# Moving the sample tile's retention behind the first gather, strips to ScalarE and a one-hot product to GpSimd

## The chip, the cores and the metric

The kernel runs on one core of one Trainium2 chip. The metric is the device time of one execution in microseconds (us), taken as the median of three runs.

## The reference

One layer of a streaming encoder is computed for two request groups that share the weights: a prompt of 1024 tokens and 8 running streams with 16 new tokens each (the "sample" group, 128 tokens), with 1024 features.

```python
h = rms_norm(x, norm1_g)
rq, rk, rv, rg, fq, fk, fv, logf = project(h, w_in, ...)   # 7 x 512 columns, and 8
ro, s_new = retention(rq, rk, rv, s0)                      # 8 heads of 64, recurrent state
fo = fox_block(...)                                        # softmax attention, 8 heads of 64
x = x + combine(ro, rg, fo, ret_out_g, fox_out_g, w_out)   # norms, swish gate on ro, w_out
x = x + peer(rms_norm(x, norm2_g), peer_wq, peer_keys, peer_u, peer_v)
...
def peer_tokens(x, wq, keys, u, v):      # per token and head: 16 experts out of 16384
    ... v1, i1 = lax.top_k(s1, 16); v2, i2 = lax.top_k(s2, 16)
    cv, ci = lax.top_k(v1 + v2 (all pairs), 16)
    e = i1[ci // 16] * 128 + i2[ci % 16]; g = softmax(cv)
    act = gelu(x . u[e]);  return sum over heads and experts of g * act * v[e]
```

For the prompt the retention state starts at zero and runs through all tokens; for the sample group each of the 8 streams starts from its own state (`state_ret`, 8 x 8 heads x 64 x 64) and returns a new one. The expert lookup needs 8 x 16 rows of `peer_u` and of `peer_v` for each of 1152 tokens: 8 KB for each expert and token, 1208 MB in all.

## The kernel before, in words

The 1152 tokens are nine tiles of 128: tiles 0 to 7 are the prompt, tile 8 (`ST`) is the sample group. The program has five parts, one after the other.

1. `phase_norm`: x is normalized and transposed to `hT` for all nine tiles, and the retention queries RQ are projected for the tiles in `EARLY`.
2. `projection([RK, RV], ...)`: retention keys and values of the tiles in `EARLY`. A projection of one tile to 512 columns is 16 matmul records on TensorE (PE).
3. `phase_retention`: scores, causal mask, outputs, state and swish gate of the tiles in `EARLY`, and the forget logits of all tiles.
4. `projection([FQ, FK, FV], ...)`: the softmax attention's q, k, v for tiles 0 to 2.
5. `phase_tail`: the rest, in two layers that run beside each other. The **stream** works token by token through all 1152 tokens. GpSimd (POOL) issues one indirect DMA per token (L1914, 1 MB each) into a ring of nine slots. VectorE (DVE) takes the dot products with u (L2842). After each four tokens ScalarE (ACT) computes a tanh (L2130) for the gelu, DVE forms the 128 x 32 x 4 block of weights called strips in two instructions (`exg` L2859, `strips` L2864), and PE multiplies it with v (L2468), which frees four ring slots (`uv_free`). The **fronts** are everything else for three groups of tiles, 0 to 2, 3 to 5, 6 to 8: projections, retention of the tiles not in `EARLY`, attention, output projection, query and key scores (rq, rscore), top-16 searches (rtop) and the choice of the experts (rcand, 27 steps per tile, rexp, rmove). Front 0 lies before the first gather; front 1 must have chosen tile 3's experts before gather 384 and front 2 tile 6's before gather 768.

Each engine's queue is in order. `front_steps()` writes the front steps down as two threads (`rest`, `choice`), each step with a cost per engine and the steps it needs. `deal()` plays the steps against a model of the stream once, when the program is built, and so fixes between which gathers, dots, tanhs and multiplications each step is put (`due`). A front step on an engine is a companion of the stream.

In the kernel before, `RETAINED = {1: [3, 4, 5], 2: [6, 7]}`: tiles 3 to 5 get their retention in front 1, tiles 6 and 7 in front 2, and `EARLY` is tiles 0, 1, 2 and 8. Tile 8 has a step of its own in `phase_retention` (`outputs_sample`, then `turn_sample`), and its new states are made in four pieces in the steps of tiles 1 and 2 (`state_sample`, `add_state`); its 128 x 512 retention output goes to HBM (`rets`) and is read back by `sload` in front 2, beside the things that the sample attention needs. The gate weights of that phase are loaded in its beginning, and tile 0's outputs come before its gate matmuls there. In the choice, for each of tiles 1 to 8 DVE four times compares the candidates with an iota to a one-hot block of 128 x 1024 (L2604), multiplies it with the positions (L2608) and sums it (L2611).

## Time and profile before

| | |
|---|---|
| median of 3 runs | 3679.78 us (3669.91 to 3693.92) |
| profiled execution, own time | 3684.22 us |
| its span, first to last instruction | 3682.4 us |
| PE / DVE / ACT / POOL busy | 64% / 66% / 13% / 38% |
| DMA moved | 1363.76 MB, 370 GB/s over the span |
| first gather issued, last gather issued | 443.8 us, 3663.2 us |

Times in the rows below are us from the start of the span unless marked ns. The profile is one execution; its own time, 1.8 us above its span, is 4.4 us above the median of the runs.

### The profile page before, as it was taken

To read this page: it belongs to the slowest core of one execution; us is meant where nothing else is said; L and a number is where in the kernel's file an instruction comes from. 1 tells how busy PE (TensorE), PEld (TensorE's weight loads), DVE (VectorE), ACT (ScalarE), POOL (GpSimd) and SP (SyncE) were. 2 spreads that over 40 slices of the span, in tenths; PEclk is the share of its full clock that TensorE was granted. 3 is DMA by queue.
4 is the path that set the end of the run, shared out by engine and by line. 5 is a ranking of instruction groups with operands and counts; after the bars stand their busy time and mean duration, and the time that the engine had idled before them with its cause. 6 is when DMAs were issued, how large, how long until landed. Compare 5 with 4: busy or idle time off the path is not lost.

```text
span 3682.4 us, 32200 instructions
## 1 busy us (share of the span) xinstructions
PE 2344.0 (64%) x10543; PEld 926.8 (25%) x10543; DVE 2422.2 (66%) x6345; ACT 494.6 (13%) x1368; POOL 1403.2 (38%) x1276
## 2 busy tenths in 40 slices
PE   7997885758677678667747877788443343334333
PEld 3544431313333233122213444233100000000000
DVE  3232479886666559888765566578988765565555
ACT  1113211011022111011101122111101100000000
POOL 0010033533444434444343344434544444444443
PEclk9998997879778789778857678799665665656555
DMA  3145289999999999999999999999999999999998
GB/s 145 41 143 199 93 346 406 413 390 401 418 407 401 409 400 415 397 408 423 401 400 404 383 384 404 417 401 414 411 403 418 419 417 418 417 420 420 417 420 370
DMA packets 227782, 1363.76 MB, mean 370 GB/s; under 512 B 34384, under 2 KB 53720, under 8 KB 76064
## 3 DMA queue, kind: packets, MB, share of 16 engines
q0 software_dynamic: 165888, 1208.03, 79.9%
q1 hardware_dynamic: 61440, 153.08, 11.0%
q8 instruction: 84, 1.38, 0.1%
q10 hardware_dynamic: 288, 0.59, 0.0%
q14 instruction: 82, 0.67, 0.0%
HBM read 1336.77 MB, written 24.85 MB: 370 GB/s over the span
## 4 chain that ended last, share of the span: by engine, by line
DMA 39%; PE 24%; DVE 13%; POOL 9%; issue 6%; ACT 1%; POOLq 0%; DVEq 0%; ACTq 0%
DMA M<-in_peer_uv,M 39%; PE yp L2468 12%; POOL M L1914 8%; DVE M L2842 6%; PE ab L2416 2%; PE ab L2233 1%; PE ab L2178 1%; PE d L2213 1%; DVE exg L2859 1%; DVE strips L2864 1%; PE ef L2450 1%; PE d L2395 1%; PE c L2201 1%; DVE gel L2851 1%; PE c L2395 1%
## 5 line engine op out<-in xcount | busy, mean ns | idle before, releaser
L1914 POOL DMA_INDIRECT M<-in_peer_uv,M x1152 | 1302.9, 1131 | 1819.6 <-PE yp L2468 1477.9
L2842 DVE SCALAR_TENSOR_TENSOR M<-M 128x1024 f32<-128x1024 f32 x1152 | 1407.7, 1225 | 780.8 <-DMA M<-in_peer_uv,M 752.7
L2468 PE MATMUL yp<-M,strips 128*32 128x512 f32 x4608 | 861.5, 886 | 1092.5 <-DVE strips L2864 1065.9
L2468 PEld LDWEIGHTS yp<-M,strips 128*32 128x32 f32 x4608 | 154.7, 141 | 1680.2 <-DVE strips L2864 1310.0
L2130 ACT ACTIVATE gel<-gel 128x4 f32<-128x4 f32 x288 | 59.2, 206 | 1997.9 <-DVE gel L2853 1979.5
L2416 PE MATMUL ab<-M 128*128 128x512 f32 x576 | 264.6, 608 | 4.1 <-ACT M L2084 4.1
L2233 PE MATMUL ab<-M 128*128 128x512 f32 x320 | 148.4, 614 | 0.0
L2416 PEld LDWEIGHTS ab<-M 128*128 128x128 f32 x576 | 107.9, 195 | 147.2 <-issue 142.7
L2291 PE MATMUL ab<-M 128*128 128x512 f32 x288 | 133.2, 614 | 5.7 <-DVEq L2635 5.6
L434 PE MATMUL z<-M 128*128 128x512 f32 x272 | 120.6, 600 | 0.9 <-PEq L105 0.9
L2656 DVE CUSTOM_DVE_ANT_0 M<-ab,M 128x896 f32<-128x896 f32 (+6 forms) x64 | 48.4, 756 | 91.4 <-PE ab L2179 70.6
L2864 DVE SCALAR_TENSOR_TENSOR strips<-gel,exg 128x128 f32<-128x128 f32 x288 | 84.1, 292 | 33.4 <-ACT gel L2130 23.2
L2201 PE MATMUL c<-ident,M 128*128 128x128 f32 x288 | 56.7, 313 | 65.4 <-ACT M L1952 41.7
L2842 DVE DVE_READ_ACCUMULATOR M<-M 128x1 f32 x1152 | 95.0, 82 | 0.0
L2859 DVE TENSOR_TENSOR exg<-e,gel 128x128 f32<-128x128 f32 x288 | 84.1, 292 | 10.0
L2213 PE MATMUL d<-M 128*64 128x128 f32 x576 | 88.7, 307 | 0.9 <-ACT M L1960 0.9
L2178 PE MATMUL ab<-M 64*128 64x512 f32 (+3 forms) x192 | 86.3, 560 | 3.8 <-DVE mins L2656 3.8
L2233 PEld LDWEIGHTS ab<-M 128*128 128x128 f32 x320 | 60.6, 197 | 87.6 <-issue 84.9
L2450 PE MATMUL ef<-M,ident 128*32 128x512 f32 x576 | 76.1, 664 | 5.7 <-ACT M L2126 3.5
L2213 PEld LDWEIGHTS d<-M 128*64 128x64 f32 x576 | 72.3, 155 | 17.3 <-issue 15.0
L2291 PEld LDWEIGHTS ab<-M 128*128 128x128 f32 x288 | 54.5, 196 | 81.5 <-issue 81.5
L1939 ACT ACTIVATE M<-M,mins 128x896 f32<-128x896 f32 (+6 forms) x64 | 49.6, 775 | 150.6 <-DVE mins L2656 146.4
(305 smaller groups left out, 2511.7 us busy)
## 6 DMA issues: line engine op xcount, KB each, us to landing
M<-in_c_win SPq DMA_DIRECT2D x20, 2048.0 KB, 11.4
M<-in_c_wq SPq DMA_DIRECT2D x12, 2048.0 KB, 12.2
M<-in_peer_uv,M POOLq DMA_INDIRECT x1152
M<-in_w_out SPq DMA_DIRECT2D x24, 512.0 KB, 8.6
M<-in_x_prompt SPq DMA_DIRECT2D x16, 512.0 KB, 11.2
x_scratch<-M SPq DMA_DIRECT2D x9, 512.0 KB
M<-x_scratch SPq DMA_DIRECT2D x9, 512.0 KB
out_y_prompt<-M SPq DMA_DIRECT2D x8, 512.0 KB
```

Source lines behind the costliest of these rows:

```text
L434: last = nc.tensor.matmul(z[n % 3][:, :], hT[:, k, t * P:(t + 1) * P], wbuf[:, slot(gi), k, :], start=(k == 0), stop=(k == KC - 1))
L1914: nc.gpsimd.indirect_dma_start(ring[n % NR], None, a["peer_uv"], bass.IndirectOffsetOnAxis(ap=idxH[:, t % 6, s // 4, s % 4:s % 4 + 1], axis=0)
L2178: nc.tensor.matmul(s[:, c:c + w], rows_q[b0:b0 + 64, r], rows_k[b0:b0 + 64, r, c:c + w], start=True, stop=c + w < width)
L2213: last = nc.tensor.matmul(Dk[b0:b0 + 64, 0:P], (vg if g else vn)[:, j, h * HD:(h + 1) * HD], pT[:, n % 2, j, :], start=(j == 0), stop=(j = ...
L2233: last = nc.tensor.matmul(half_ab[j % 2], l_h[i][:, k, :], pw[q % 2][:, k, :], start=(k == 0), stop=(k == KC - 1))
L2291: last = nc.tensor.matmul(half_ab[j % 2], l_h[i][:, k, :], f_pw(q)[:, k, :], start=(k == 0), stop=(k == KC - 1))
L2416: last = nc.tensor.matmul(half_ab[i % 2], xT[:, tt, k, :], wq(g, b)[:, k, :], start=(k == 0), stop=(k == KC - 1))
L2450: last = nc.tensor.matmul(EF[32 * b:32 * b + 32, half, :], ident[:, 32 * j:32 * j + 32], xb[:, 512 * half:512 * half + 512], start=True, s ...
L2468: last = nc.tensor.matmul(yp[32 * j:32 * j + 32, 512 * c:512 * c + 512], strips[:, n % 2, j, :], ring[(4 * n + j) % NR][:, D + 512 * c:D + ...
L2842: nc.vector.scalar_tensor_tensor(out=row, in0=row, scalar=1.0, in1=xrep[:, s % 4, :], op0=ALU.mult, op1=ALU.mult, accum_out=dots[:, t % 2, ...
L2859: link(nc.vector.tensor_tensor(exg[:, :, :], bc(e32[:, :].unsqueeze(1), [P, 4, 32]), bc(g[:, 3, :].unsqueeze(2), [P, 4, 32]), ALU.mult))
L2864: nc.vector.scalar_tensor_tensor(out=strips[:, n % 2], in0=bc(g[:, 2, :].unsqueeze(2), [P, 4, 32]), scalar=1.0, in1=exg[:, :, :], op0=ALU. ...
```

## The change

Tile 8's retention leaves the phases ahead of the tail and becomes part of front 2: `RETAINED[2]` is 6, 7, 8 and `EARLY` is 0, 1, 2. Its projections are four more `lmm` steps, its scores an `lsc`; its outputs come in two halves from an initial state loaded from HBM in another layout (`lxo`), are turned back (`lback`), and its new states are made in four pieces (`lvbd`, `lnew`) and written to HBM by ACT's queue. The sample attention's small loads move into the second `sload`, behind the last state piece, while the first two pieces of its key and value caches keep their place ahead of the outputs. `rets` goes. In `phase_retention` tile 0's gate matmuls come before its outputs, and the weights FQ are loaded in its beginning. In the stream the strips are made by ACT, in four activations of 128 x 32 with a scale from memory, after one 128 x 4 instruction of DVE. In the choice of tiles 1 to 8 the product L2608 goes to POOL; DVE waits for it (`picked`) before the sum. Some semaphores are merged, and the planner's costs are adapted. The diff, cut to its core:

```diff
-        RETAINED = {1: [3, 4, 5], 2: [6, 7]}
+        RETAINED = {1: [3, 4, 5], 2: [6, 7, 8]}
...
                 for s, t in enumerate(ORDER):
-                    whole = s == 0 or t == ST
...
-                    if t == ST:
-                        outputs_sample()
...
+                def across(half):
+                    add(rest, ("lxo", g, half), pe=(6.1, ("sp", ("sload", g, 0)), ("dve", ("lsc", g, NL - 1)), ("act", ("lval", g, 3 * NL - 1)),
+                                                    *(bank("A", "act", ("lxo", g, 1)) if half == 0 else [])),
+                        **({"act": (0.7, ("pe", ("lxo", g, 1)))} if half else {}))
+                def renew(r):
+                    add(rest, ("lnew", g, r), pe=(1.3, ("dve", ("lvbd", g, r)), *bank("DB"[r % 2], "dve", ("lnew", g, r))),
+                        dve=(1.2, ("pe", ("lnew", g, r)), ("pe", ("lxo", g, 1))), act=(0.3, ("dve", ("lnew", g, r))))
...
+                if len(prompt) < NL:
+                    across(0)
+                    gated(0, "lout")
+                    across(1)
+                    renew(0)
+                    gated(1, "lout")
+                    add(rest, ("lback", g), pe=(0.75, ("act", ("lxo", g, 1)), *bank("C", "act", ("lback", g))), act=(1.5, ("pe", ("lback", g))))
+                    renew(1)
+                    spread(2)
+                    gated(2, "lback")
+                    renew(2)
+                    spread(3)
+                    renew(3)
...
+                    if g == SG:
+                        routed += [("dve", ("lnew", g, PAIRS - 1))]
...
-                        add(rest, ("sprep", g, p), dve=(1.3, ("sp", ("sload", g, 0))))
+                        add(rest, ("sprep", g, p), dve=(1.3, ("sp", ("sload", g, 1))))
...
+                        if p in PICKED:
+                            add(choice, ("rcand", g, i, p), pool=(2.2, ("dve", ("rcand", g, i, p - 1))))
...
+                    elif kind == "lxo":
+                        half, n = arg[0], NKEPT[g] + len(RETAINED[g])
...
+                        for h in range(4 * half, 4 * half + 4):
+                            b0, r = 64 * (h % 2), h // 2
+                            o = four(half_ab[0])[b0:b0 + 64, r, :]
+                            nc.tensor.matmul(o, l_v[-1][:, h * HD:(h + 1) * HD], l_sT[-1][:, h % 2, r, :], start=True, stop=False)
+                            for b in range(NB):
+                                c = slice(b * NS, (b + 1) * NS)
+                                last = nc.tensor.matmul(o[:, c], l_s0[r][b0:b0 + 64, b, :], l_qT[-1][b0:b0 + 64, r, c],
+                                                        start=False, stop=(b == NB - 1))
...
                 def gelu_tanh(n):
                     act.wait_ge(gel1, n + 1)
                     nc.scalar.activation(gel[:, n % 2, 2, :], gel[:, n % 2, 1, :], ACT.Tanh).then_inc(gel2, 1)
...
+                    if n >= 2:
+                        act.wait_ge(uv_free, n - 1)
+                    act.wait_ge(gel3, n + 1)
+                    for j in range(4):
+                        last = nc.scalar.activation(strips[:, n % 2, j, :], e32[:, :], ACT.Copy, scale=gel[:, n % 2, 3, j:j + 1])
+                    last.then_inc(strip_done, 1)
...
-                    link(nc.vector.tensor_tensor(exg[:, :, :], bc(e32[:, :].unsqueeze(1), [P, 4, 32]),
-                                                 bc(g[:, 3, :].unsqueeze(2), [P, 4, 32]), ALU.mult))
                     dve.wait_ge(gel2, n + 1)
-                    if n >= 2:
-                        dve.wait_ge(uv_free, n - 1)
-                    nc.vector.scalar_tensor_tensor(out=strips[:, n % 2], in0=bc(g[:, 2, :].unsqueeze(2), [P, 4, 32]),
-                                                   scalar=1.0, in1=exg[:, :, :], op0=ALU.add, op1=ALU.mult
-                                                   ).then_inc(strip_done, 1)
+                    nc.vector.scalar_tensor_tensor(out=g[:, 3, :], in0=g[:, 2, :], scalar=1.0, in1=g[:, 3, :],
+                                                   op0=ALU.add, op1=ALU.mult).then_inc(gel3, 1)
```

## Rows read from the trace of the kernel before

**Rows 1.** Busy times by stage: three stretches of five parts, us.

```profile
69.20:129.20 60.00, 58.81 (x144) 26.31 (x144) 10.95 (x20) 4.69 (x8) 0.00 (x0) 0.97 0.09 35
...
129.20:216.50 87.30, 82.13 (x470) 42.04 (x470) 32.66 (x55) 9.13 (x16) 7.87 (x9) 0.98 0.31 88
...
644.00:3682.40 3038.40, 1818.80 (x8496) 681.57 (x8496) 2119.17 (x5425) 367.73 (x1046) 1292.73 (x1149) 0.73 0.99 407
```

**Rows 2.** DMA queues from the first gather to the end: packets, MB, share.

```profile
q0 software_dynamic: 165888, 1208.03, 90.8%
q1 hardware_dynamic: 30480, 102.69, 8.0%
```

**Rows 3.** The chain of waits late in the stream: start, us, what.

```profile
3220.14 10.05 DMA M<-in_peer_uv,M
...
3232.61 3.68 PE yp L2468 x16
```

**Rows 4.** PE's timeline where the first part ends and the second begins.

```profile
55.87 8.80 PE L298 MATMUL z<-M 128*128 128x512 f32 x16 [0.83 <-ACT M L194]
...
69.26 1.40 PE L434 MATMUL z<-M 128*128 128x512 f32 x2 [0.93 <-PEq L105]
```

**Rows 5.** PE's timeline in the retention phase.

```profile
135.14 1.89 PE L686 MATMUL op<-M 128*128 128x64 f32 x16
...
139.62 7.13 PE L759 MATMUL z<-M 128*128 128x512 f32 x16 [1.98 <-DMA M<-in_c_win]
146.69 1.16 PE L673 MATMUL sc<-M 64*128 64x128 f32 x16
...
169.61 1.16 PE L673 MATMUL sc<-M 64*128 64x128 f32 x16
...
180.73 1.08 PE L741 MATMUL opT<-M 128*64 128x512 f32 x4
...
183.92 1.58 PE L741 MATMUL opT<-M 128*64 128x512 f32 x4 [1.05 <-DVE M L841]
```

**Rows 6.** DMA queue q1 from 188 to 207 us (new states written).

```profile
q1 hardware_dynamic: 4435, 1.56, 33.0%
```

**Rows 7.** Groups of instructions in the stream by line and shape.

```profile
L2864 DVE SCALAR_TENSOR_TENSOR strips<-gel,exg 128x128 f32<-128x128 f32 x288 | 84.1, 292 | 33.4 <-ACT gel L2130 23.2 <-DVE exg L2859 0.9
L2859 DVE TENSOR_TENSOR exg<-e,gel 128x128 f32<-128x128 f32 x288 | 84.1, 292 | 10.0
...
L2130 ACT ACTIVATE gel<-gel 128x4 f32<-128x4 f32 x288 | 59.2, 206 | 1997.9 <-DVE gel L2853 1979.5 <-issue 17.9
...
L2857 DVE SCALAR_TENSOR_TENSOR gel<-dots,M 128x4 f32<-128x4 f32 x288 | 44.8, 156 | 0.0
...
L2608 DVE TENSOR_TENSOR M<-M 128x1024 f32<-128x1024 f32 x34 | 41.5, 1221 | 0.2
```

**Rows 8.** Groups of POOL over the whole span.

```profile
L1882 POOL TENSOR_TENSOR psm<-psm,nhalf 128x8 f32<-128x8 f32 x12 | 23.9, 1992 | 1.0
...
L888 POOL MEMSET M<- 128x512 f32 x1 | 0.5, 524 | 77.3 <-POOLq L105 77.3
```

**Rows 9.** Busy times in two stretches where the experts are routed.

```profile
1343.00:1743.00 400.00, 275.15 (x1132) 103.10 (x1132) 339.58 (x1108) 56.47 (x160) 171.31 (x151) 0.83 1.00 412
...
2412.00:2641.00 229.00, 158.00 (x654) 61.66 (x652) 191.66 (x628) 27.33 (x72) 96.91 (x86) 0.85 1.01 413
```

**Rows 10.** POOL's timeline, gather 384.

```profile
1564.06 1.01 POOL L1914 DMA_INDIRECT M<-in_peer_uv,M  x1 [2.82 <-ACT M L1966]
```

**Rows 11.** ACT's timeline, tile 6's experts moved.

```profile
2636.74 4.27 ACT L1966 CAST M<-M 32x32 int32<-32x32 f32 x16
```

**Rows 12.** POOL's timeline, gather 765 (gather 768 is the third after it).

```profile
2686.95 0.95 POOL L1914 DMA_INDIRECT M<-in_peer_uv,M  x1 [4.31 <-PE yp L2468]
```

**Rows 13.** Retention projections of front 2: count, first and last start.

```profile
L2233 PE MATMUL ab<-M x128: 592/592/1223, 1737.9 to 1841.0; 128*128 128x512 f32 x128
```

**Rows 14.** PE's timeline, third piece of the sample's keys.

```profile
1936.22 1.97 PE L2330 MATMUL ab<-ident,M 128*128 128x128 f32 x8 [7.48 <-DMA M<-in_c_ck]
```

More of the change, by code:

```diff
@@ L678, in outputs @@
                 def outputs(t):
-                    s = AT[t]
                     o = op[t % 2]
@@ L2617, in choose @@
                                             ).then_inc(csub, 1)
-                chosen = {}
+                chosen, taken = {}, [0]
                 def front(step):
```

512 lines of the change are left out of this document (251 added, 261 removed).

## The prediction

> **What bounds the kernel now.** I read the busy times by stage first. The span falls in two. Ahead of the first gather, to 443.8 us, PE is the full engine: it is busy 58.8 of 60.0 us in the key and value projections and 82.1 of 87.3 us in the retention phase, with the DMA engines at 0.09 and 0.31 [rows 1]. From 644 us on the DMA share is 0.99 at 407 GB/s, while PE is busy 60% and DVE 70% [rows 1]. Next the DMA queues over the stream's 3238.6 us: the gathers alone hold the 16 engines 90.8% of it, 2941 us, and everything else 8.0%, 259 us [rows 2]. That leaves about 39 us, or 1.2%, for idling and small descriptors. So the stream lasts as long as its bytes do, whatever DVE and PE have spare. The chain of waits says it in its way: late in the stream the last gather of four takes 10.05 us from issue to landing, and PE begins 2.4 us after that [rows 3]; four gathers take 2941/288 = 10.2 us of engine time, so these 10 us are queueing behind other gathers, not distance. Work that is taken from DVE in the stream buys no time by itself. Work that is taken from before the first gather buys all of it, as long as it fits beside the stream.
>
> **The part ahead of the gathers.** First part: tile 8's queries, from 55.87 to 69.26 us [rows 4]. Without them the second part can start once the last transposes are copied (at 55.9) and after the 0.9 us that the border costs: 56.8. This saves 12.4 us. Second part: 8 projections take 60.0 us, 7.5 each with the border [rows 1]; 2 go, and the matmuls themselves take 7.13 + 0.2 at most in the third part [rows 5], so I take 14.6 us. Third part: tile 8's step goes, from 146.69 to 169.61, 22.9 us. Four state pieces go, in two pairs: 1.08 + 1.05 (wait) + 1.58 us, twice, 7.4 us in all [rows 5]. Against that, tile 0's outputs, from 135.14 until PE sat idle at 139.62 - 1.98 = 137.64, 2.5 us, lay in the shade of the load of the gate weights [rows 5]. Now the gate matmuls come first and still wait for that load, and the outputs come after: 2.5 us are given back. Net 27.8 us. The 1 MB of old states and 1 MB of new ones also leave this phase; nothing waited for them, so this is worth nothing here. DVE is busy 33 of 87 us there and can't be next [rows 1]; the weights FQ now come earlier and were not waited for. Sum: 12.4 + 14.6 + 27.8 = **54.8 us**, by which the first gather should come earlier, at about 389 us. Front 0 itself is unchanged.
>
> **What the stream gets: bytes.** New in it: 1.05 MB of old states, 0.52 MB of tile 8's hT, 0.07 MB of constants, less 0.26 MB of `rets`, some 1.4 MB. The other transfers of the stream cost 259 us for 102.7 MB, 2.5 us a MB [rows 2]: 3.5 us. The new states are written in 256-byte pieces: when they were written before, with two `rets`, 4435 packets held the engines 33.0% of 19 us, 6.3 us [rows 6]; 4096 of them are the states, so 5.8 us. The ends are 3.5 us (by bytes alone) and 6.3. Together **+9.3 us** (7 to 10), and these are not hidden, because the engines are full.
>
> **Strips on ACT.** DVE loses two instructions of 0.292 us and gains one like L2857, 0.156 [rows 7]: 0.43 us per group of four tokens, 123 us over 288 groups. ACT gains four activations. The nearest rows are 0.206 us (128x4) and 4.27 us for 16 of 32x32, 0.267 each [rows 7, 11], so 0.8 to 1.1 us a group, some 270 us in all, on an engine that is busy 12% of the stream. On the path from the last dot to PE it adds 0.6 us (0.16 + 0.85 in place of strips' 0.29, less overlap; 0.3 to 1.2). The cover is the queueing of rows 3: when a batch of four is issued, a gather or two is still being moved. I cost it at 0 in the steady state. ACT's queue now holds its next front step behind the wait for DVE's small instruction (`gel3`) and for `uv_free`; both are due within a microsecond of the tanh, which it waited for already. Without the cover it would be 0.6 x 288 = 173 us, which is why the fullness of the DMA matters so much.
>
> **The product on POOL.** It takes 32 x 1.22 = 39 us from DVE [rows 7]. On POOL no row shows a multiplication of 1024. L888 writes 512 numbers in 0.52 us, 1.02 ns each [rows 8]; one pass gives 1.05 us, two reads and a write 3.1 us, and I take 2.2, as one read port's two passes are nearer than either end. L1882 takes 1.99 us for 8 numbers [rows 8], but that is a power. POOL's pause ahead of a batch is 4.31 us in the row of gather 765 [rows 12], so the product fits. Behind it on POOL are gathers, behind the wait for it on DVE are dots. Each engine is in order, so a late batch makes DVE wait for POOL, which waits for PE, up to some microseconds, of which the ring takes the most: 0 to 1 us each, **+3 us** in all (0 to 30). The Trainium skill (GPSIMD Engine Reference, Performance versus the Vector engine) has a two-input tensor_tensor of 2048 fp32 at 4497 ns on GpSimd against 2293 on VectorE. By that it would be an estimated 2.25 us here, and the sum stays as it is; DVE's row, 1.22 us, agrees with its half of the pair.
>
> **Does the last front still come in time?** This decides the rest. Before, the experts of tile 6 are in place at 2636.74 + 4.27 = 2641.0 us, and gather 768, the first to need them, is issued three gathers of 0.95 + 0.3 us after 2686.95, at 2690.7 [rows 11, 12]: 50 us of slack. Tile 3's come with none, gather 384 waits 2.8 us for them [rows 10]. Added to front 2: four `lmm`; the eight of before took 103.7 us, 13.0 each, and no more than one goes into a group of 10.2 us [rows 13]: 41 to 52 us. Two halves of outputs: tile 8's step of 22.9 us holds them beside gate matmuls of 7.1 and scores of 1.2 [rows 5], so they are 14 us at most, and one half fits between two multiplications of the stream: two groups, 20 to 25 us. Four state pieces, each a ping-pong of DVE, PE, DVE, partly side by side: three to six groups, 30 to 60 us. The small loads now start behind them; but the sample attention's third key piece came only at 1936.22, 7.5 us late [rows 14], and that one is queued behind the same values as before, so 0 to 25 us. Together 90 to 160 us, and I take 95, near the lower end, because a state piece is short on PE (1.08 us when its operands are there, [rows 5]) and several fit into one group. Against that: the 9.3 us of bytes delay gather 768 as well; and DVE, busy 85% from 1343 to 1743 and 84% from 2412 to 2641 [rows 9], is what rtop and the choice wait for there, and in the stream's beginning too. Its relief is 0.43 us a group over the 62 groups of these stretches and some 30 of the beginning, 39 us, and 1.22 x 4 for each tile chosen on the way, some 10 us more if POOL keeps up. So front 2 would be later by 95 - 49 = 46 us against the stream, and slack and bytes make 60. It just fits: no stall in the likeliest case, but with a margin of 14 us under an uncertainty of 40.
>
> **The sum.** 3684.2 - 54.8 + 9.3 + 3 = 3641.7 us for the profiled execution; less the 4.4 us by which that stood above the median, 3637. With a few us for idling that a fuller ACT lets through I say **3639 us**.
>
> **Rivals.**
> *The last front is late* (tile 6's experts come after the ring asks for them). For it: the additions above to 160 us and a relief that may be less than 49 if PE, busy 69% in both stretches, sets the pace instead of DVE. Against: 50 us of slack. Point from which it costs: front 2 later by over 60 us. Late by 90, it costs 30 us: 3669. Slower than before begins at about 100 us; at 160 less 20 of relief, 140, the gathers stand still for 80 us, all engines with them: 3719 (+1.1%). That is the case of the other side.
> *POOL and DVE wait for one another.* Here the products are paid with DMA idling. For it: 32 new hand-overs, where L1882's twelve are of the same kind [rows 8]. At 1 us each instead of 0.1: 3639 + 29 = 3668. The Trainium skill (GPSIMD Engine Reference, Specifications) names VectorE instructions with two SBUF inputs as contending with GpSimd, and each dot is one; by that rule the product would stretch by what is left of a dot, 1.2 us, here.
> *The front doesn't shrink as said*, because a load or a barrier holds a part: against it, the DMA share there is 0.09 and 0.31 [rows 1]. Half of the 54.8 us: 3666.
> *Better than forecast*: front 1 no longer late, less idling of the 39 us left over: -10 us, 3627.
>
> **Chances.** Forecast, with up to 5 us either side, 0.42; better 0.10; late front 0.23 with stalls to 45 us and 0.08 beyond; POOL 0.12; front 0.05. A measurement of this kernel can tell about 1%, 37 us: faster by more than that is below 3643. The forecast is mostly there (0.38 of its 0.42), with the better case 0.48, and 0.02 of the others: 0.50. Slower by over 1%, above 3717: half of the last 0.08 and a little, 0.06. Within: 0.44. The range leaves out the long tail of the late front and half of the better case: 3624 to 3692.
>
> **What would show it.** The first gather at 389 us (385 to 394) shows the first sum. 288 groups of four ACT records at 0.2 to 0.25 us, and DVE's L2864 gone, show the strips; the distance from the last dot's landing to PE, 2.4 us, should be 3.0, with gathers still 10 us from issue to landing late in the stream. POOL's product between 1.1 and 3.1 us, and DVE's idle time before its sum under 1 us in the mean, show the third part. Gather 768 should come after POOL's usual wait for PE, not for ACT's moves; if it waits for ACT, the late front is true, and DMA's share falls for that long. The prediction is wrong above all if front 2's relief isn't there, or if the span from first gather to end, 3238.6 us before, grows by more than 20 us.

## The result, and the profile after

The changed kernel takes **3723.35 us** in the median of its four runs, 41 us more than the kernel before beside it (3682.01 us). One run of the four took 8446 us; it is in that median (without it, 3718.52 us) but not in the ratio, which is 1.0108, 95% interval 1.0082 to 1.0133, or some 40 us. Forecast were 3639 us, with a range of 3624 to 3692. The profiled execution took 3714.63 us, its span is 3712.6 us.

The front phases did what was forecast, and a little more. PE's stages for the two remaining projections and for the retention phase, then everything from 585 us on, as rows 1 show it for before (us from start to end and length; PE, PEld, DVE, ACT, POOL busy; clock, DMA share, GB/s):

```profile
56.40:100.50 44.10, 42.93 (x109) 19.23 (x110) 8.20 (x15) 3.51 (x6) 0.06 (x1) 1.00 0.13 48
100.50:159.30 58.80, 54.23 (x268) 27.05 (x268) 18.75 (x32) 6.73 (x12) 5.98 (x7) 0.97 0.21 77
585.00:3712.60 3127.60, 1887.81 (x8746) 722.02 (x8744) 2041.12 (x5145) 626.37 (x2145) 1331.99 (x1181) 0.75 0.98 396
```

The second part takes 44.1 us instead of 60.0, the retention phase 58.8 instead of 87.3 [rows 1]. But the last line is the trouble: 396 GB/s where the kernel before had 407, so the DMA engines, which set the length of the stream, are less full. The queues from the first gather to the end say the same (compare [rows 2]):

```profile
q0 software_dynamic: 165888, 1208.03, 89.0%
q1 hardware_dynamic: 31056, 103.59, 7.8%
q10 hardware_dynamic: 4224, 1.05, 0.1%
```

The same 1208.03 MB of gathered rows hold the engines 89.0% of the stream instead of 90.8%. The stream, from the first gather to the end, is 3327.6 us long instead of 3238.6. Of these 89 us some 61 are idle time of the engines, 8 are the other queues' packets, and 20 are gathered packets that take longer (89.0% of 3327.6 is 2961 us, against 2941 before for the same bytes). In the run with only the retention moved they take 2940 us; why they take longer here is not shown. Where does it fall behind? One row of the gathers' line for each stretch gives the number of gathers in it and the start of its last: 257 gathers, 449, 769 and 865 (counted from 0, the last ones are gathers 256, 448, 768 and 864). First the changed kernel, then the kernel before:

```profile
L1858 POOL DMA_INDIRECT M<-in_peer_uv,M x257: 932/938/2106, 385.0 to 1147.9; - x129
...
L1858 POOL DMA_INDIRECT M<-in_peer_uv,M x449: 932/945/2106, 385.0 to 1753.7; - x150
...
L1858 POOL DMA_INDIRECT M<-in_peer_uv,M x769: 932/944/2106, 385.0 to 2708.0; - x193
...
L1858 POOL DMA_INDIRECT M<-in_peer_uv,M x865: 932/944/2106, 385.0 to 2964.5; - x173
```

```profile
L1914 POOL DMA_INDIRECT M<-in_peer_uv,M x257: 932/938/1974, 443.8 to 1181.5; - x129
...
L1914 POOL DMA_INDIRECT M<-in_peer_uv,M x449: 932/940/2018, 443.8 to 1751.5; - x150
...
L1914 POOL DMA_INDIRECT M<-in_peer_uv,M x769: 932/940/2021, 443.8 to 2691.6; - x193
...
L1914 POOL DMA_INDIRECT M<-in_peer_uv,M x865: 932/946/2021, 443.8 to 2937.9; - x173
```

The first gather is issued 58.8 us earlier. Gather 256 is only 33.6 us ahead, gather 448 is 2.2 us behind, gather 864 is 26.6 us behind. I call what is lost since the first gather the lag: 25 us at gather 256, 61 at 448, 75 at 768, 85 at 864, and 88 at the last (1151). After gather 864 next to nothing is added; there no front is dealt into the stream any more. So the loss is no price per group of four tokens, and not one stall: it gathers in the stretches where VectorE has front work.

The new parts, by line (busy, mean ns of one; then idle time before them and who ended it):

```profile
L2098 ACT ACTIVATE strips<-e,gel 128x32 f32<-128x32 f32 x1152 | 276.1, 310 | 105.1 <-DVE gel L2884 102.6 <-issue 2.4
...
L1839 POOL TENSOR_TENSOR M<-M 128x1024 f32<-128x1024 f32 x32 | 77.9, 2435 | 47.0 <-DVEq L2608 46.7
...
L2884 DVE SCALAR_TENSOR_TENSOR gel<-gel 128x4 f32<-128x4 f32 x288 | 46.8, 163 | 101.4 <-ACT gel L2091 97.7 <-DVE gel L2881 2.0 <-issue 1.7
```

The sizes were forecast well: 276 us for the strips, 2.4 us for a product. The idle columns were not. POOL stands 46.7 us in front of the products, and gathers stand behind it. VectorE waits 97.7 us for the tanh, where `exg` used to cover that time; in the run with only the retention moved, which keeps the old strips, its wait there is 22.7 us. So 75 of the 123 us that the strips took off VectorE came back as waiting.

How long a group holds its slots is seen in the chain of waits late in the stream (start us, us, what):

```profile
3298.86 10.07 DMA M<-in_peer_uv,M
3308.96 1.24 DVE M L2864 x2
3310.22 0.17 DVE gel L2873
3310.42 0.17 DVE gel L2875
3310.61 0.21 ACT gel L2091
3310.92 0.17 DVE gel L2884
3311.18 0.97 ACT strips L2098 x4
3312.19 3.69 PE yp L2470 x16
3315.87 0.26 issue
3316.13 0.94 POOL M L1858
```

The transfer is 10.07 us from issue to landing here too, as in [rows 3]. PE begins at 3312.19, 3.3 us after the landing, against 2.4. From the end of a group's fourth dot to PE's first matmul the median of the 288 groups is 2.01 us, against 1.18 in the kernel before. From the end of the same dot to the end of the group's last matmul, when the slots come free, the mean is 5.85 us, against 4.73.

### The profile page after: what moved, and what is told of

The parts are those of the page before. It is cut to its first block, busy times and chain, and to the rows that moved or that the text cites. A ratio compares the mean times of both kernels' runs of the same rounds, so it can differ in the third digit from the quotient of the medians.

```text
span 3712.6 us, 33319 instructions
## 1 busy us (share of the span) xinstructions
PE 2360.2 (64%) x10537; PEld 943.5 (25%) x10537; DVE 2321.3 (63%) x6025; ACT 762.8 (21%) x2520; POOL 1441.2 (39%) x1308
## 3 DMA queue, kind: packets, MB, share of 16 engines
q0 software_dynamic: 165888, 1208.03, 79.8%
## 4 chain that ended last, share of the span: by engine, by line
DMA 35%; PE 23%; DVE 15%; POOL 8%; issue 6%; ACT 5%; SPq 0%; DVEq 0%; ACTq 0%; another core or an unknown queue 0%; POOLq 0%
DMA M<-in_peer_uv,M 34%; PE yp L2470 11%; POOL M L1858 7%; DVE M L2864 7%; ACT strips L2098 3%; PE ab L2418 2%; PE ab L2201 1%; PE ab L2146 1%; DVE gel L2875 1%; PE d L2181 1%; DVE M L2618 1%; DVE gel L2873 1%; DVE M L2605 1%; PE c L2397 1%; DMA M<-out_new_fox_v_s 1%
## 5 line engine op out<-in xcount | busy, mean ns | idle before, releaser
L1858 POOL DMA_INDIRECT M<-in_peer_uv,M x1152 | 1263.2, 1097 | 1786.6 <-PE yp L2470 1457.5
L2864 DVE SCALAR_TENSOR_TENSOR M<-M 128x1024 f32<-128x1024 f32 x1152 | 1439.3, 1253 | 827.3 <-DMA M<-in_peer_uv,M 807.4
L2098 ACT ACTIVATE strips<-e,gel 128x32 f32<-128x32 f32 x1152 | 276.1, 310 | 105.1 <-DVE gel L2884 102.6
L2418 PE MATMUL ab<-M 128*128 128x512 f32 x576 | 263.5, 605 | 4.1 <-ACT M L2045 4.1
L2201 PE MATMUL ab<-M 128*128 128x512 f32 x384 | 176.8, 613 | 0.0
L2418 PEld LDWEIGHTS ab<-M 128*128 128x128 f32 x576 | 107.3, 194 | 148.3 <-issue 143.8
L2293 PE MATMUL ab<-M 128*128 128x512 f32 x288 | 135.9, 623 | 4.1 <-DVEq L2642 4.1
L2884 DVE SCALAR_TENSOR_TENSOR gel<-gel 128x4 f32<-128x4 f32 x288 | 46.8, 163 | 101.4 <-ACT gel L2091 97.7
L433 PE MATMUL z<-M 128*128 128x512 f32 x240 | 105.0, 593 | 1.4 <-PEq L105 1.4
L2201 PEld LDWEIGHTS ab<-M 128*128 128x128 f32 x384 | 73.0, 196 | 108.0 <-issue 107.6
L1839 POOL TENSOR_TENSOR M<-M 128x1024 f32<-128x1024 f32 x32 | 77.9, 2435 | 47.0 <-DVEq L2608 46.7
```

Source lines behind the costliest of these rows:

```text
L433: last = nc.tensor.matmul(z[n % 3][:, :], hT[:, k, t * P:(t + 1) * P], wbuf[:, slot(gi), k, :], start=(k == 0), stop=(k == KC - 1))
L1839: nc.gpsimd.tensor_tensor(o4, o4, bc(f4[:, q // 16:q // 16 + 4, half, :].unsqueeze(2), [P, 4, TOPK, TOPK]), ALU.mult).then_inc(picked, 1)
L1858: nc.gpsimd.indirect_dma_start(ring[n % NR], None, a["peer_uv"], bass.IndirectOffsetOnAxis(ap=idxH[:, t % 6, s // 4, s % 4:s % 4 + 1], axis=0)
L2098: last = nc.scalar.activation(strips[:, n % 2, j, :], e32[:, :], ACT.Copy, scale=gel[:, n % 2, 3, j:j + 1])
L2201: last = nc.tensor.matmul(half_ab[j % 2], l_h[i][:, k, :], pw[q % 2][:, k, :], start=(k == 0), stop=(k == KC - 1))
L2293: last = nc.tensor.matmul(half_ab[j % 2], l_h[i][:, k, :], f_pw(q)[:, k, :], start=(k == 0), stop=(k == KC - 1))
```

## Each part alone

Three parts were changed, so I took them apart in both directions. Theory A put the loss on the product, because all 32 products lie where the lag grows; B on the strips; C on the moved retention's own loads.

**Product back on VectorE**, in the changed kernel:

```diff
-        PICKED = range(15, 27, 3)
+        PICKED = ()
...
-                            if few:
+                            if few or not PICKED:
```

> The changed kernel with one part undone: VectorE multiplies the one-hot itself again in every tile; strips stay on ScalarE, tile 8's retention stays in the last front. Theory A (the product on GpSimd is what cost): the changed kernel's gathers fall behind those of before by 13 us between gathers 64 and 128, by 34 us between 352 and 448 and by 16 us between 736 and 864, and all 32 products lie before gathers 81 to 121, 353 to 429 and 745 to 833; GpSimd waited 46.7 us for the one-hots in them. Undone, some 50 to 63 us come back: 3660 to 3675 us. Theory B (the strips on ScalarE are what cost, by the longer path to TensorE and by ScalarE's queue): VectorE takes back 32 products of 1.2 us, nothing else moves: 3710 to 3730 us. Theory C (the loads and stores of the moved retention cost): 3710 to 3730 us too.

**Strips back on VectorE**, in the changed kernel: ScalarE's four activations go, `exg` and the `strips` product return in `weigh`, and the planner has its old costs.

```diff
-                    for j in range(4):
-                        last = nc.scalar.activation(strips[:, n % 2, j, :], e32[:, :], ACT.Copy, scale=gel[:, n % 2, 3, j:j + 1])
...
-                        free[e] += 0.55
+                        free[e] += 1.0
```

> The changed kernel with one part undone: the strips on VectorE again (exg and one product), with the planner's old costs for them; the product stays on GpSimd. Theory A (the product is what cost): VectorE has 0.43 us more in each of 288 groups beside a stream that DMA bounds: 3715 to 3735 us, no gain. Theory B (strips on ScalarE are what cost; 0.6 us more from the last dot to TensorE in 288 groups is up to 173 us where it shows): a good part comes back, 3660 to 3690 us. Theory C: 3715 to 3730 us.

**Both back**, so that only the retention is moved (both edits):

> Only the moved retention is left of the change: strips and product on VectorE, old costs in the planner. Theory A: what the product cost (50 to 63 us) comes back, the strips neither cost nor gave: 3660 to 3675 us. Theory B: 3650 to 3680 us, with most of the difference from the run with only the product undone. Theory C (the moved retention's own transfers and the late sample loads cost): no better than 3700 us, though the first gather is at 385 us instead of 444.

Then, on the kernel before, **the strips alone on ScalarE** and **the product alone on GpSimd** (the same edits the other way round).

> The kernel before with one part of the change: the strips on ScalarE, with the planner's new costs for them. Theory D/E (a path longer by 1.1 us in the mean and ScalarE's queue eat the ring's slack): it cost 36 us on top of the moved retention, and there some 20 us of it were given back because the last front was no longer late at gather 768; in the kernel before gather 768 has 50 us of slack, so nothing is given back: 3715 to 3740 us. Rival G (the strips cost only in company with the moved retention, whose steps crowd ScalarE): 3680 to 3695 us.

> The kernel before with one part of the change: the product on GpSimd for tiles 1 to 8 (two semaphores of loads merged to make room). Theory W (GpSimd and VectorE wait for each other, 32 times, with gathers queued behind): 26 us with strips on VectorE, 37 us with strips on ScalarE were measured on top of the moved retention: 3705 to 3725 us here. Rival (VectorE's relief of 39 us of work counts where its queue holds the dots): 3670 to 3685 us.

| kernel | median us | ratio to before (95%) |
|---|---|---|
| changed kernel | 3723.4 | 1.0108 (1.0082 to 1.0133) |
| product back | 3687.3 | 1.0001 (0.9979 to 1.0022) |
| strips back | 3677.0 | 0.9980 (0.9962 to 0.9997) |
| both back: moved retention alone | 3651.3 | 0.9901 (0.9871 to 0.9930) |
| strips alone | 3725.5 | 1.0123 (1.0092 to 1.0154) |
| product alone | 3716.8 | 1.0090 (1.0059 to 1.0122) |

A ratio compares a kernel with runs of the kernel before taken beside it, so it can differ from the quotient of two medians in this document by some 5 us. At 3682 us the ratios are -36 us for the moved retention (its median says -32), +45 for the strips and +33 for the product. Their sum is +42, and together they measured +40. Each has an interval of some 11 us either way, so the parts add up as far as this can be told; agreement to 2 us is luck. Theory A was too narrow: by the ratios the product back gave 39 us and not 50 to 63, and the strips back gave 47, which A had called no gain. B alone fell as well. C fell: with the moved retention alone the time is the best of all. Rival G fell too; the strips cost without the moved retention.

The lag, worked out from the issue times of the gathers in each trace (against gather 0 of the same trace, less the same for before, us):

| gather | changed | strips alone | product alone | retention alone |
|---|---|---|---|---|
| 256 | 25 | 9 | 13 | -1 |
| 448 | 61 | 32 | 41 | -1 |
| 736 | 69 | 36 | 22 | 7 |
| 768 | 75 | 38 | 23 | 28 |
| 864 | 85 | 39 | 29 | 23 |
| 1151 | 88 | 39 | 29 | 24 |

## Why the product costs

Two mechanisms were open: the waits (each engine stands in order until the other has come), or the work on GpSimd itself. **Handoff** keeps the waits and takes the work away; it stands on the kernel with retention moved and strips on VectorE, so its marks are 3677 us (full product on GpSimd) and 3651 (none). VectorE does the multiplication itself after the wait, and the planner is told so.

```diff
                         pool.wait_ge(one_hot, 4 * (t - 1) + c + 1)
-                        nc.gpsimd.tensor_tensor(o4, o4, bc(f4[...]), ALU.mult).then_inc(picked, 1)
+                        pool.sem_inc(picked, 1)
...
                                 dve.wait_ge(picked, taken[0])
+                                dl(nc.vector.tensor_tensor(o4, o4, bc(f4[...]), ALU.mult))
```

> Moved retention and strips on VectorE (3677 us with the product on GpSimd, 3651 us with it on VectorE), and of the product on GpSimd only the two waits: GpSimd waits for the one-hot and signals at once, without multiplying; VectorE waits for the signal and multiplies itself. Theory W (the waits cost: GpSimd stands in front of gathers until VectorE reaches a one-hot, VectorE stands until GpSimd gets there): 3670 to 3685 us, the 26 us stay. Rival O (GpSimd's 2.4 us of own work ahead of the gathers costs, or a port that both engines want): 3650 to 3660 us, the 26 us go.

Measured: 3672.0 us, 0.9966 (0.9950 to 0.9982). The waits alone cost 21 us, where waits and work cost 26. The split is weak, since the interval of the full product is 0.9962 to 0.9997. And they don't cost in the same place. Handoff's lag at gather 352 is 9 us and at gather 384 31 us, because that gather, the first to need tile 3's experts, stands for them (2.8 us before [rows 10]):

```profile
1536.21 0.94 POOL L1858 DMA_INDIRECT M<-in_peer_uv,M  x1 [16.72 <-ACT M L1910]
```

Gather 768 stands 23.37 us for tile 6's, against 19.67 with the retention alone. These two make 17.6 of the 23 us by which handoff's last gather is behind that kernel's. So much of what hand-overs cost there is a longer choice of experts in a front that had no slack. With the product on GpSimd and the strips on VectorE neither gather waits for experts; GpSimd waits 24.3 us for the one-hots instead, VectorE 38.2 us for the products. Handoff shows that hand-overs alone can cost this much, and not that they are the same 21 us. Here is one, in POOL's timeline of the changed kernel:

```profile
1437.04 0.98 POOL L1858 DMA_INDIRECT M<-in_peer_uv,M  x1 [0.30 <-issue]
1438.33 0.95 POOL L1858 DMA_INDIRECT M<-in_peer_uv,M  x1 [0.30 <-issue]
1442.38 3.43 POOL L1839 TENSOR_TENSOR M<-M 128x1024 f32<-128x1024 f32 x1 [3.10 <-DVEq L2608]
1451.34 2.34 POOL L1839 TENSOR_TENSOR M<-M 128x1024 f32<-128x1024 f32 x1 [5.54 <-DVEq L2608]
1453.83 1.79 POOL L1858 DMA_INDIRECT M<-in_peer_uv,M  x1
```

From 1439.28 to 1453.83 no gather is issued, 14.5 us, in which 5.7 gathers' worth of DMA time (2.55 us each, from rows 2) would pass. GpSimd stands at its second product 5.54 us, until VectorE has made dots, a weighing and the next one-hot.

The work on GpSimd has a row too. VectorE's timeline at the second of these products, and at another:

```profile
1449.99 1.22 DVE L2605 TENSOR_TENSOR M<-M,iota 128x1024 f32<-128x1024 f32 x1
1451.35 3.41 DVE L2864 SCALAR_TENSOR_TENSOR M<-M 128x1024 f32<-128x1024 f32 x1
...
2776.88 3.42 DVE L2864 SCALAR_TENSOR_TENSOR M<-M 128x1024 f32<-128x1024 f32 x1
2780.22 0.08 DVE L2864 DVE_READ_ACCUMULATOR M<-M 128x1 f32 x1
2780.22 1.21 DVE L2864 SCALAR_TENSOR_TENSOR M<-M 128x1024 f32<-128x1024 f32 x1
```

The dot that starts with the product takes 3.41 us in place of 1.22: it ends 1.1 us after the product does, as if it had begun only about then. In the changed kernel 28 of the 32 products hold a VectorE instruction up by 1.1 to 2.8 us, a 128x4 one by 2.0 as well (2.19 in place of 0.16), together 61 us (each instruction beside a product, less the median of its line). Beside the other four VectorE ran nothing. The product took 39 us off VectorE and put 61 on it. In the run with strips back 20 products hold VectorE up, 47 us for the 39. What this alone costs in time no run shows, since every kernel with the product on GpSimd has the hand-overs as well.

The hold depends on the instruction, and on who is first. From the run with strips back, POOL's row and then VectorE's:

```profile
1459.07 3.43 POOL L1840 TENSOR_TENSOR M<-M 128x1024 f32<-128x1024 f32 x1 [9.89 <-DVEq L2601]
```

```profile
1459.08 1.23 DVE L2857 SCALAR_TENSOR_TENSOR M<-M 128x1024 f32<-128x1024 f32 x1
...
1460.30 0.28 DVE L2517 FIND_INDEX8 M<-M 128x8 uint32<-128x128 f32 x1
...
1461.66 1.92 DVE L2857 SCALAR_TENSOR_TENSOR M<-M 128x1024 f32<-128x1024 f32 x1
```

Here the dot goes first and it is the product that takes 3.43 us in place of 2.35; then the steps of a search run beside the product at their usual 0.28 us; the next dot, with two inputs again, is held. The Trainium skill (SBUF — State Buffer, SBUF: two separate sides) calls the port pair that the two engines share "an exclusive lock, not a bandwidth split"; the trace agrees. The twelve small powers of L1818 (1.68 us) held nothing up.

**Fewer products.** In the run with only the moved retention, gather 768 waits 19.7 us for tile 6's expert numbers. If relief of VectorE was worth its price anywhere, it was there: the product on GpSimd for tile 6 alone, then for tiles 6 to 8.

```diff
-                        if p in PICKED:
+                        if p in PICKED and G0[g] + i in ON_POOL:      # ON_POOL = (6,), then (6, 7, 8)
```

> Moved retention, strips on VectorE, and the product on GpSimd for tile 6 alone (four products), where in the run with only the moved retention (3651 us) gather 768 waits 19.7 us for this tile's expert numbers while VectorE works off the tile's selection with no dots between. Theory L (the last front is late at gather 768, and the relief is worth its waits only there): 3636 to 3646 us. Rival (four products' waits cost as much as they give): 3648 to 3658 us.

> As the run with tile 6 alone, with the product on GpSimd for tiles 6 to 8 (twelve products). Theory W: each product beyond tile 6 costs 0.5 to 1 us (18 us for the twenty of tiles 1 to 5), so 4 to 8 us over the run with tile 6 alone: 3642 to 3654 us. Rival (what is left of the product's cost lies in tiles 1 to 5 only): the same as the run with tile 6 alone.

Measured: 3660.8 us (0.9947, 0.9931 to 0.9964) and 3665.1 (0.9953, 0.9939 to 0.9968), both slower than 3651 without any. The first lies above both ranges named beforehand; the second differs from it by less than the intervals. Theory L fell in this form. The profile of the first shows the reason: the selection is a chain of one-hot, product, sum. GpSimd's product is 1.1 us longer than VectorE's own, and behind each product VectorE has a dot (3.45 us, held up by it), steps of a search and a weighing in its queue before it gets to the sum and the next one-hot. POOL's timeline, with no gather between 2648.2 and 2673.1, 24.9 us in place of 19.67:

```profile
2656.63 2.37 POOL L1840 TENSOR_TENSOR M<-M 128x1024 f32<-128x1024 f32 x1 [5.76 <-DVEq L2601]
2666.33 2.34 POOL L1840 TENSOR_TENSOR M<-M 128x1024 f32<-128x1024 f32 x1 [7.33 <-DVEq L2601]
2673.11 0.98 POOL L1859 DMA_INDIRECT M<-in_peer_uv,M  x1 [4.45 <-ACT M L1911]
```

## Why the strips cost

Theory D: the path from dot to free slots is longer, and the ring's slack was what took up late dots. E: ScalarE's queue, where front steps now stand behind strips. F: the planner's new costs. Two kernels put four small activations (128x1, 0.19 us each, where those of the strips take 0.31) with the strips' waits into ScalarE's queue while VectorE still makes the strips; they differ only in whether TensorE waits for them. Base: moved retention alone, 3651 us.

```diff
+                    if n >= 2:
+                        act.wait_ge(uv_free, n - 1)
+                    act.wait_ge(strip_done, n + 1)
+                    act.wait_ge(gel3, n)
+                    for j in range(4):
+                        last = nc.scalar.activation(idle[:, j:j + 1], e32[:, j:j + 1], ACT.Copy, scale=1.0)
+                    last.then_inc(gel3, 1)
...
-                    pe.wait_ge(strip_done, n + 1)
+                    pe.wait_ge(gel3, n + 1)          # the relay only
```

> The kernel with only the moved retention (3651 us): VectorE makes the strips as before, but ScalarE then runs four small activations on spare columns, behind the same wait for the slots as in the changed kernel, and TensorE waits for these instead of for the strips. The path from the last dot of a group to TensorE grows by about 1 us (in the changed kernel it grew from 1.18 to 2.01 us in the median, 1.74 to 2.86 us in the mean), and VectorE is not relieved. Theory D (the longer path takes the slack of the ring of nine slots, so each delay of a dot reaches the DMA queue earlier): 3680 to 3700 us, as the strips on ScalarE did (3687 us), or a little more, as VectorE has its strips still. Rival E (the strips on ScalarE cost by occupying ScalarE's queue, where the front's steps stand behind them): the same time, but then the run in which TensorE does not wait for these activations is as slow. Rival F (the planner's other costs dealt the front worse): 3648 to 3658 us.

> As the run with the relay over ScalarE, with the same four activations and the same waits in ScalarE's queue, but TensorE waits for VectorE's strips as before. Theory D (path length): 3648 to 3660 us, as without them (3651 us). Rival E (ScalarE's queue): 3680 to 3700 us. Rival F (planner): 3648 to 3658 us, as theory D, and the relay run the same.

**The same load without its waits** (those for `uv_free` and `strip_done` taken out):

> The run in which ScalarE does four idle activations per group that nobody waits for (3664 us, against 3651 us without them), now without their waits for the strips and for the slots: they follow the tanh at once. If ScalarE's standing in the wait costs: 3648 to 3655 us. If its being busy for 0.9 us a group costs: 3660 to 3668 us.

**The strips alone, with the planner's old costs**:

> The kernel before with the strips on ScalarE (3725 us with the planner's new costs), but with the planner's old costs for a group, so that every front step stands where it stood in the kernel before. Rival F (the new costs, 0.55 us for a group on VectorE where it takes longer, deal the front too densely): 3695 to 3710 us. Theory D/E (path and queue): 3718 to 3730 us.

**A ring of eight** on the moved retention alone, to price the slack:

```diff
-        NR = 9
+        NR = 8
```

> The kernel with only the moved retention (3651 us), with a ring of eight slots for the gathered rows in place of nine (in the gathers, the dots, TensorE's reads and the planner alike). Each group's four slots must then be free one gather, some 2.5 us, earlier for the DMA queue to stay full. Theory D (what counts is the time from a group's last dot to its slots coming free against the ring's slack, where VectorE's front steps delay dots; 1.1 us more of it cost 28 to 45 us): 60 to 100 us more, 3710 to 3750 us. Rival (the ring has slack to spare, and the strips cost through ScalarE's queue and the dealing alone): 3651 to 3665 us.

| kernel | median us | ratio (95%) | last dot to free slots, mean us |
|---|---|---|---|
| moved retention alone | 3651.3 | 0.9901 (0.9871 to 0.9930) | 4.73 |
| activations, nobody waits, no waits | 3658.0 | 0.9934 (0.9911 to 0.9956) | 4.75 |
| activations with waits | 3664.7 | 0.9938 (0.9918 to 0.9958) | 4.79 |
| activations as a relay | 3678.7 | 0.9988 (0.9973 to 1.0004) | 5.26 |
| strips alone | 3725.5 | 1.0123 (1.0092 to 1.0154) | 5.72 |
| strips alone, old costs | 3717.1 | 1.0091 (1.0067 to 1.0115) | 5.58 |
| ring of eight | 3835.9 | 1.0416 (1.0391 to 1.0440) | 4.74 |

No single theory holds. Standing in ScalarE's queue costs 13 us, 7 of them without the waits; the intervals overlap with that of no activations and with each other, so both figures are weak. Making TensorE wait for the same instructions costs 14 us more, and here the intervals are apart, for a path that is longer by 0.47 us: 30 us per us. On the kernel before, with the planner's old costs, the strips lengthen the path by 0.85 us. By that slope some 25 us are path, with the queue's 13 it makes 38, and 34 were measured (ratio 1.0091). The planner's new costs would be the other 11 of the 45, but there too the intervals overlap. These shares are sums, not a single run, and that the slope holds from 0.47 to 0.85 us is assumed. Over the wider step below it is steeper: the ring of eight takes away one gather's time, 2.55 us, and costs 185 us, 72 us per us and far beyond my 60 to 100. Even late in the stream, with no front beside it, its queue is no longer full: its gathers' share from 2900 us to the end, then that of the ring of nine.

```profile
q0 software_dynamic: 48859, 355.71, 96.4%
```

```profile
q0 software_dynamic: 42155, 306.92, 99.0%
```

So in quiet stretches the slack lies between 1.1 us (the changed kernel adds some 3 us of lag after gather 864) and 2.55. In the stretches where VectorE works on the front, less is left of it.

**Freeing the slots in pairs** was to give that slack back in the changed kernel, and, as a control, in the moved retention alone: TensorE's matmuls in the order of rows 0, 0, 1, 1, then 2, 2, 3, 3, a signal after the first half, and the first two gathers of a batch waiting for that half.

```diff
+                            u, v = (j // 2 + 2 * c, j % 2)
...
+                        elif c == 0:
+                            last.then_inc(uv_half, 1)
...
+                        pool.wait_ge(uv_half, (n - NR) // 4 + 1)
+                    if n >= NR and (n - NR) % 4 == 2:
```

> The changed kernel (3723 us) with its slots freed in two pairs per group: TensorE takes rows 0 and 1 first and signals after half of its 16 matmuls, GpSimd's first two gathers wait for that half alone, some 1.8 us earlier. Strips stay on ScalarE, the product on GpSimd. Theory D (both parts cost by eating the ring's slack): the 1.1 us of path are more than made up, and part of the product's waits: 3665 to 3690 us. Rival (the strips cost by ScalarE's queue, the product by holding GpSimd in its wait, where an earlier free slot is of no use): 3712 to 3725 us.

> The kernel with only the moved retention (3651 us), with its slots freed in two pairs per group as in the run before this. Its DMA queues are idle for some 45 us in all, 15 of them at the start and 20 at gather 768, and neither is a wait for a slot. Theory D: 3 to 12 us better at most, 3639 to 3648 us. Rival (the pairs help or hurt as such, by the other order of matmuls or by another wait per group on GpSimd): below 3635 us or above 3655 us.

Measured: 3723.6 us (1.0096, 1.0076 to 1.0116) and 3655.0 (0.9912, 0.9885 to 0.9939), no gain in either. It tells nothing of theory D, because no slot came free earlier. PE's and POOL's timelines of the second kernel:

```profile
3226.60 3.32 PE L2466 MATMUL yp<-M,strips 128*32 128x512 f32 x16 [6.28 <-DVE strips L2884]
```

```profile
3230.21 0.99 POOL L1861 DMA_INDIRECT M<-in_peer_uv,M  x1 [3.95 <-PE yp L2466]
3231.51 0.95 POOL L1861 DMA_INDIRECT M<-in_peer_uv,M  x1 [0.30 <-issue]
```

The 16 matmul records end at 3229.92 and the first gather goes out 0.29 us later, not at the half, 3228.6. In the trace the record that carries the half's signal is the 14th of the 16 to start, in all 286 groups between the first and the last, and the signal comes 0.09 us before the full one (median). The records start in four waves of four, at 0.00, 0.86, 1.71 and 2.56 us, in this order as in the old one. The strips are 32 columns wide and go to four different column groups; the waves read as one pass of each group at a time, whatever row the program names first. The Trainium skill (TensorE: Matmul & The Clock Gate, Part 3) describes small tiles as running concurrently in the array, and the waves agree. It also has matmuls start and end in the program's order, and here the trace does not agree: the signal on the fourth of the eight matmuls that kernel.py names comes with the last wave. That theory D was wrong is not shown, and its confirmation by giving slack back is missing.

## Why the moved retention gave 36 and not 45

In the run with only the retention moved, POOL's timeline where the last front hands over (the fourth gather is number 768):

```profile
2640.79 1.90 POOL L1859 DMA_INDIRECT M<-in_peer_uv,M  x1 [0.30 <-issue]
2642.99 0.95 POOL L1859 DMA_INDIRECT M<-in_peer_uv,M  x1 [0.30 <-issue]
2663.61 0.95 POOL L1859 DMA_INDIRECT M<-in_peer_uv,M  x1 [19.67 <-ACT M L1911]
```

The last front is late: 19.67 us of wait, in place of 50 us of slack [rows 11, 12]. The account closes with it: the first gather of this kernel is issued at 387.8 us, 56.0 earlier; from there on the packets of all queues take 6.6 us more than before and the engines idle 17.2 us more; that leaves the 32.2 us by which the span is shorter. In the changed kernel gather 768 waits 0.30 us, because the strips and the product had slowed the gathers by more than the front was late. VectorE there stands once for 26 us inside the sample attention, at a scan, and the wait is put down to the sample rows of V. Two kernels took these loads off the scan's wait, on a semaphore of their own:

```diff
-...rearrange("b n h d -> n b (h d)")).then_inc(sc_in, 16)
+...rearrange("b n h d -> n b (h d)")).then_inc(vn_in, 16)
...
-                        dve.wait_ge(sc_in, 16 * (NB + 6))
+                        dve.wait_ge(sc_in, 16 * (NB + 4))
```

> The changed kernel with the loads of the sample rows of V on a semaphore of their own, waited for by TensorE where it first uses them, as in the kernel before; VectorE's scan waits only for what it reads. In the changed kernel's trace that scan waits 26.1 us for them, in order ahead of all dots, and the gathers fall behind by 18 us between 480 and 512. Theory C (these loads cost): 15 to 20 us come back, 3703 to 3710 us. Theory A or B alone: the ring refills and the wait is made up, 3718 to 3728 us. If the loads ahead of them in the same queue end as late, nothing changes either: the scan then waits for those.

> The kernel with only the moved retention (3651 us), with the loads of the sample rows of V on a semaphore of their own. There gather 768 waits 19.7 us for the expert numbers of tile 6, the first tile of the last front. Theory L (the last front is late, and that is what keeps the moved retention from its full gain): the scan's wait for these loads lies in the last front's own chain, so this front ends up to 20 us earlier and the wait at gather 768 shrinks: 3632 to 3642 us. Rival (the wait has cover in the front and only moves to a later step, the cache loads or the state's stores): 3646 to 3654 us.

Measured: 3718.5 us (1.0085, 1.0054 to 1.0115), and 3651.5 (0.9915, 0.9885 to 0.9944). Nothing changes: the scan waits nearly as long for another input, 22.9 us for 26.1 in the changed kernel, 26.8 for 26.7 with the moved retention alone. VectorE's wait in the changed kernel, then in the second of the two:

```profile
DVE M L2774 <- DMA M<-out_new_fox_v_s: 26.1, 1, 26.1
```

```profile
DVE M L2767 <- DMA M<-lft_scratch: 26.8, 1, 26.8
```

The releaser named is only the last of a batch; the batch as a whole is late, behind the last piece of the new states. **Eager dealing** was the other try, the planner's cost of a group at 0.55 us with nothing else changed:

> The kernel with only the moved retention (3651 us), with the planner's cost of a group on VectorE at 0.55 us in place of 1.0 us and nothing else: front steps are dealt earlier against the dots. Theory L2 (the dealing sets the 20 us wait at gather 768): the wait shrinks, and if the denser front costs nothing on the way, 3635 to 3645 us. Rival F (denser dealing delays dots): 3655 to 3670 us, even where the wait goes.

Measured: 3654.8 us (0.9933, 0.9912 to 0.9955), with POOL's longest wait for the moved experts still 19.8 us. So neither the batch's last load nor this cost sets the lateness. Which of the steps added to the front does is left open, and the 26 us wait itself isn't excluded, since neither edit took it away; moving the small loads ahead of the state pieces wasn't tried, since their place in memory is still used by the retention then.

## Right and wrong, step by step

- **The front ahead of the gathers**: forecast 54.8 us and a first gather at 389 us; measured 385.0, 58.8 us earlier. Right, slightly low (12.8, 15.9 and 28.5 us in the three parts, for 12.4, 14.6 and 27.8; 1.6 more behind them).
- **Bytes, +9.3 us**: right in size. The packets of all other queues from the first gather on take 272 us of engine time in the changed kernel, against 264, so 8.
- **Strips, 0 us**: the step that failed most. They cost 45 us alone, some 34 with the planner's old costs. The path grew by 0.83 us in the median (0.6 forecast) and the relief of 123 us fell to 48, but the error was the cover. "The cover is the queueing of rows 3" was read late in the stream, where it is true: no lag comes there. It was then taken as valid for the stretches of [rows 9], where VectorE is 85% busy. The prediction named the price without cover, 173 us, and set it at zero instead of at a share.
- **The product, +3 us (0 to 30)**: mis-sized; 33 us. Its duration was right (2.4 us for 2.2). "0 to 1 us each" for the hand-overs was 21 us in 32 on the one base where it was taken apart, inside that range but seven times the 3 us; some 14 of them fell on gather 384, whose experts the prediction itself had found to come with no slack [rows 10] and then left out of the product's price. The relief of 39 us was none, since VectorE's dots and weighings are held up during a product. The rival said 29 us for the hand-overs, 1.2 us of stretch and 3668 us; it had the mechanism and nearly the price, and the stretch was 2.2 us.
- **The last front just fits**: wrong on the moved retention alone, by 19.7 us at gather 768, well inside its rival's price; in the changed kernel it is hidden behind the other losses, so that the sign to look for, a wait for ScalarE's moves, was absent although the time was far off.
- **The sum**: -54.8 + 9.3 + 3 gave -42.5. Measured are -36 (retention), +45 and +33. Of the 84 us of error 45 are the strips and 30 the product. The prediction's own sign of failure, more than 20 us added from the first gather to the end, is met with 89.
- **The case of the other side** was put on the late front. It came from two parts that were to relieve VectorE and were priced at nearly nothing.

Of all that ran, the moved retention alone is the fastest, 0.9901 of before (0.9871 to 0.9930), with its variants within the interval; the changed kernel is among the slowest.

## What to carry over

A ring in front of a full DMA queue has a slack that can be measured: take one slot away. Here 2.55 us of it cost 185 us, so any step between the last use of a slot and its release is on the path, however idle the engine that does it, and "DMA-bound" read in a quiet stretch doesn't cover a busy one. Relief of an engine was worth nothing here, where the work went to one that issues the transfers in order and that holds the relieved engine up while it works. And when a change has several parts, forecast each against zero with its own worst case: three parts added up here, to +42 us for a measured +40, each with some 11 us of uncertainty.

## What the runs showed of the hardware

- A GpSimd product of 128x1024 fp32 (2.36 us) holds a two-input VectorE instruction up by 1.1 to 2.8 us, in 28 cases of 32 in the changed kernel and 20 of 32 with strips back, even one of 128x4. Steps of a search (FIND_INDEX8, 0.28 us) aren't held, and small powers of 128x8 hold nothing up.
- TensorE runs matmuls of 32 columns into four column groups side by side, in four waves 0.86 us apart, in either program order; a signal after half of them comes 0.09 us before the end's.
- Four activations of 128x32 with a scale from memory take 0.96 us together; each record is 0.31 us long, so they overlap.
